# Reordering the two ends of a Strassen-style MLP whose down products share one PSUM bank pair

## The reference, cut to what matters

```python
D_MODEL, SEQ, DEPTH, D_FF = 1024, 512, 2, 4096

def squared_relu_mlp(h, w1, w2):
    return jnp.square(jax.nn.relu(h @ w1)) @ w2

def reference(x, mem, ...):
    for i in range(DEPTH):
        h = rmsnorm(x, norm_mix_g[i])
        x = x + (pool_mixer(h, ...) if i % 2 == 0 else sgu_mixer(h, ...))
        h = rmsnorm(x, norm_mem_g[i])
        x = x + mem_attention(h, rmsnorm(mem, norm_memkv_g[i]), ...)
        h = rmsnorm(x, norm_ffn_g[i])
        x = x + squared_relu_mlp(h, ffn_w1[i], ffn_w2[i])
    return rmsnorm(x, final_norm_g)
```

## Time and profile before

| what | value |
|---|---|
| median of 3 runs | 1170.44 us (1170.16 to 1172.05) |
| profiled execution | 1171.35 us, its span 1169.3 us |
| PE busy | 1140.8 us, 98% of the span |
| DVE busy | 829.2 us, 71% |
| ACT busy | 635.7 us, 54% |
| chain that ended last | PE 82%, DVE 9%, DMA 3%, ACT 3%, issue 2% |

### The profile page before, as it was taken

The page is one execution under the profiler, slowest core; times in us unless marked ns, Lnnn a source line. Parts: engine busy times, 40 slices in busy tenths (PEclk is TensorE's granted clock), DMA queues, the critical chain, the costliest instruction groups (busy, mean ns, idle before and its releaser), DMA issues.

```text
span 1169.3 us, 16188 instructions
## 1 busy us (share of the span) xinstructions
PE 1140.8 (98%) x6556; PEld 1003.9 (86%) x6556; DVE 829.2 (71%) x933; ACT 635.7 (54%) x773; POOL 251.3 (21%) x211
## 2 busy tenths in 40 slices
PE   8999999999999999999999999999989999999997
PEld 6888888989999999788888888888989999999975
DVE  7787647677786786777487656655757678677778
ACT  7664434765555655545444432543576656556555
POOL 0040035113012121113164044004511211112020
PEclk9999999999999999999999999999999999999999
DMA  9523134969789777735232622313587977977673
GB/s 349 206 80 101 55 135 107 244 133 192 196 181 201 186 143 164 174 73 198 91 97 84 216 91 72 108 36 144 118 227 158 198 191 179 207 171 154 146 133 102
DMA packets 48457, 176.59 MB, mean 151 GB/s; under 512 B 5504, under 2 KB 5632, under 8 KB 47744
## 3 DMA queue, kind: packets, MB, share of 16 engines
q0 software_dynamic: 18432, 67.12, 31.9%
q1 hardware_dynamic: 28368, 104.35, 26.5%
q10 hardware_dynamic: 1584, 4.10, 1.0%
HBM read 173.45 MB, written 2.10 MB: 150 GB/s over the span
## 4 chain that ended last, share of the span: by engine, by line
PE 82%; DVE 9%; DMA 3%; ACT 3%; issue 2%; POOL 0%; SPq 0%; DVEq 0%; ACTq 0%; POOLq 0%
PE psum L1874 11%; PE psum L1876 11%; PE psum L1875 11%; PE psum L2149 8%; PE psum L2150 8%; PE psum L2151 8%; PE psum L2129 8%; PE psum L2131 7%; PE psum L2130 7%; DVE w_lo L1181 2%; DMA w_raw<-in_up 2%; DMA w_raw<-in_weights 1%; DVE w_lo L1170 1%; PE psum L2066 1%; ACT w_hi L725 1%
## 5 line engine op out<-in xcount | busy, mean ns | idle before, releaser
L1181 DVE TENSOR_TENSOR w_lo<-w_sum,w_hi 128x1024 fp32r<-128x1024 f32 x112 | 136.5, 1223 | 84.2 <-ACT w_hi L725 83.9
L2149 PE MATMUL psum<-w_lo,slot_hi 128*128 128x512 f32 x448 | 176.3, 394 | 5.2 <-DVE y_rows L1519 5.2
L2150 PE MATMUL psum<-w_hi,slot_hi 128*128 128x512 f32 x448 | 176.3, 393 | 0.0
L2151 PE MATMUL psum<-w_hi,slot_lo 128*128 128x512 f32 x448 | 175.6, 392 | 0.0
L725 ACT ACTIVATE w_hi<-w_sum 128x1024 fp32r<-128x1024 f32 x112 | 117.7, 1054 | 79.8 <-PE psum L2151 76.0
L2129 PE MATMUL psum<-xs_s_lo,w_hi 128*128 128x256 f32 x512 | 145.4, 284 | 0.9 <-DVE a L1457 0.8
L2131 PE MATMUL psum<-xs_s_hi,w_lo 128*128 128x256 f32 x512 | 144.9, 283 | 0.0
L2130 PE MATMUL psum<-xs_s_hi,w_hi 128*128 128x256 f32 x512 | 144.8, 283 | 0.0
L1827 POOL DMA_DIRECT2D w_sum<-in_down x64 | 55.4, 866 | 373.5 <-DVE w_lo L1181 373.5
L1181 DVE TENSOR_TENSOR w_lo<-w_raw,w_hi 128x1024 fp32r<-128x1024 f32 x80 | 101.0, 1265 | 48.7 <-ACT w_hi L725 48.4
L725 ACT ACTIVATE w_hi<-w_raw 128x1024 fp32r<-128x1024 f32 x80 | 83.9, 1056 | 80.0 <-PE psum L2131 64.1
(11 more groups left out here) (226 smaller groups left out, 2701.1 us busy)
## 6 DMA issues: line engine op xcount, KB each, us to landing
w_raw<-in_weights SPq DMA_DIRECT2D x90, 512.0 KB, 3.7
w_sum<-in_down POOLq DMA_DIRECT2D x64, 512.0 KB, 6.9
w_sum<-in_down SPq DMA_DIRECT2D x48, 512.0 KB, 4.5
w_raw<-in_up POOLq DMA_DIRECT2D x48, 512.0 KB, 6.4
w_raw<-in_up SPq DMA_DIRECT2D x32, 512.0 KB, 3.9
up<-in_up SPq DMA_DIRECT2D x16, 512.0 KB, 4.3
up<-in_up POOLq DMA_DIRECT2D x16, 512.0 KB, 7.2
x<-in_x_t SPq DMA_DIRECT2D x2, 1024.0 KB, 8.8
```

The lines of the kernel that those rows point to most:

```text
L1181: dve.tensor_tensor(w_lo[:, c % RING, :], buffer(kind, SUM_BUFFER[STAGE[p][0]] + half), w_hi[:, c % RING, :].bitcast(F32), ALU.subtract).t ...
L2149: pe.matmul(to, s_hi[:, k, tok], w_lo[:, c % RING, cols], start=first, stop=False, skip_group_check=True)
L2150: pe.matmul(to, s_hi[:, k, tok], w_hi[:, c % RING, cols], start=False, stop=False, skip_group_check=True)
L2151: last = pe.matmul(to, s_lo[:, k, tok], w_hi[:, c % RING, cols], start=False, stop=(kp == 1 and j == 1), skip_group_check=True)
```

## The change

There are four parts. (1) In block 0, on VectorE, `c11`, the halves of `c12` and those of `c22` each move ahead of one weight split. On ScalarE the squares of a12 and a22 move behind the next weight split. SyncE issues its first DMAs of the MLP in another order. (2) The up products of block 3 are done sooner: at the end of block 2 the order was D2P6, U3P6, D2P7, U3P7, D2P4, U3P4, and it is now U3P6, D2P6, U3P7, U3P4, D2P7, D2P4 (`LAST_UPS`). The work on a12, a22, a21 and the sums s1 to s4 moves with them, and the read of D2P4 moves into the last block. (3) In the last block D3P3 gets bank pair A for itself instead of adding onto D3P5 in pair Y. (4) So D3P5 is read a second time, into the quarter of `y_rows` that D3P3 belongs to. The halves of the tile-by-tile read of D3P5 are gone. The count of matmuls, of weight chunks and of bytes is the same.

```diff
+LAST_UPS = (("D", "P1"), ("U", "P1"), ("D", "P2"), ("U", "P2"), ("D", "P5"), ("U", "P5"), ("D", "P3"), ("U", "P3"),
+            ("U", "P6"), ("D", "P6"), ("U", "P7"), ("U", "P4"), ("D", "P7"), ("D", "P4"))
-LAST_READS = ("P1", "P5", "P3", "P6", "P2", "P7", "P4")
+LAST_READS = ("P1", "P5", "P5 again", "P3", "P6", "P2", "P7", "P4")
...
-    for b in range(FB - 1):
+    for b in range(FB - 2):
         for p in ORDER:
             steps += [("D", b, p, h) for h in range(2)] + [("U", b + 1, p, h) for h in range(2)]
+    steps += [(kind, FB - 2 + (kind == "U"), p, h) for kind, p in LAST_UPS for h in range(2)]
...
 def rows_pair(b, p):
-    return PAIR_E if (b, p) == (FB - 1, "P2") else ROWS_PAIR[p]
+    if b == FB - 1 and p in ("P2", "P3"):
+        return PAIR_E if p == "P2" else PAIR_A
+    return ROWS_PAIR[p]
...
@@ SyncE, start of an MLP @@
-                refill(l, "U", 0, "P2")
                 sp.wait_ge(lo_ready, N.lo[f"xs{l}", "P4"] + 1)
-                for name in ("11", "22"):
-                    for half in range(2):
-                        quarter(l, "D", 0, name, half)
-                refill(l, "U", 0, "P7")
+                for half in range(2):
+                    quarter(l, "D", 0, "11", half)
                 refill(l, "U", 0, "P4")
+                refill(l, "U", 0, "P2")
+                for half in range(2):
+                    quarter(l, "D", 0, "22", half)
+                refill(l, "U", 0, "P7")
@@ ScalarE, block 0 @@
-                squared(0, 1, a12, "P6")
                 ahead("U", 0, "P7", 1)
+                squared(0, 1, a12, "P6")
+                ahead("U", 0, "P4", 0)
                 operand(0, "P2", a12, h=1)
-                ahead("U", 0, "P4", 0)
+                ahead("U", 0, "P4", 1)
                 squared(0, 2, a22, "P7")
-                ahead("U", 0, "P4", 1)
@@ ScalarE, end of block 2 @@
+                ahead("D", b, "P7", 0)
+                last_quarter(c)
+                ahead("D", b, "P7", 1)
+                ahead("D", b, "P4", 0)
+                operand(c, "P2", a12, h=1)
+                ahead("D", b, "P4", 1)
                 b = FB - 1
-                last_quarter(b)
@@ VectorE, end of block 2 @@
+                ahead("U", c, "P4", 1)
+                ahead("D", b, "P7", 0)
+                sum_s1(c)
+                ahead("D", b, "P7", 1)
+                sum_s3(c)
+                sum_s2(c)
+                ahead("D", b, "P4", 0)
+                read(b, "P7")
+                operand(c, "P2", a12)
+                ahead("D", b, "P4", 1)
+                sum_s4(c)
                 b = FB - 1
-                sum_s1(b)
                 ahead("D", b, "P1", 0)
-                sum_s3(b)
                 operand(b, "P5", s1)
+                read(b - 1, "P4")
                 ahead("D", b, "P1", 1)
-                sum_s2(b)
-                sum_s4(b)
+                operand(b, "P3", a12)
                 ahead("D", b, "P2", 0)
-                operand(b, "P3", a12)
                 read(b, "P1")
                 ahead("D", b, "P5", 0)
-                read(b, "P5", tile_waits=True)
                 ahead("D", b, "P5", 1)
                 operand(b, "P6", a11)
                 ahead("D", b, "P3", 0)
+                read(b, "P5")
                 ahead("D", b, "P3", 1)
+                read(b, "P5", again=True)
                 read(b, "P3")
@@ TensorE, end of block 2 @@
+                kept_done(c, "P1")
+                up_product(c, "P6")
+                read_done(b, "P1")
+                down_product(b, "P6")
+                sum_done(c, "P6")
+                up_product(c, "P7")
+                pe.wait_ge(sum_half, 3 * l + 3)
+                up(c, "P4", 0)
+                sum_done(c, "P7")
+                up(c, "P4", 1)
+                read_done(b, "P6")
+                down_product(b, "P7")
+                read_done(b, "P7")
+                down_product(b, "P4")
                 b = FB - 1
                 read_done(b - 1, "P4")
                 down_product(b, "P1", fresh=True)
                 kept_done(b, "P3")
                 down(b, "P2", 0, fresh=True).then_inc(psum_ready, 1)
                 read_done(b - 1, "P3")
                 down_product(b, "P5", fresh=True)
-                waits = [read_count(l, b, "P5", t) for t in range(2)]
-                down(b, "P3", 0, tile_waits=waits).then_inc(psum_ready, 1)
-                down(b, "P3", 1).then_inc(psum_ready, 1)
+                kept_done(b, "P4")
+                down_product(b, "P3", fresh=True)
                 read_done(b, "P1")
```

More of the change, by code:

```diff
@@ L593, in read_count @@
         order = LAST_READS if b == FB - 1 else READS
-        return 14 * (FB * l + b) + 2 * order.index(p) + t + 1
+        return 14 * (FB * l + b) + 2 * l + 2 * order.index(p) + t + 1
     TOK = (slice(0, NMEM), slice(NMEM, S))
@@ L1015, in mlp @@
                     ahead("U", c, "P4", 1)
+                ahead("U", c, "P6", 0)
+                keep_p3(c)
+                ahead("U", c, "P6", 1)
+                ahead("D", b, "P6", 0)
+                ahead("D", b, "P6", 1)
+                squared(c, 1, a12, "P6")
+                ahead("U", c, "P7", 0)
+                operand(c, "P1", a11, h=0)
+                ahead("U", c, "P7", 1)
+                ahead("U", c, "P4", 0)
+                squared(c, 2, a22, "P7")
+                ahead("U", c, "P4", 1)
[5 more added lines that the diff above has]
+                ahead("D", b, "P4", 1)
                 b = FB - 1
-                last_quarter(b)
                 ahead("D", b, "P1", 0)
@@ L1499, in sum_s4, with read @@
                                              op1=ALU.subtract).then_inc(s_step, 1)
-                def read(b, p, tile_waits=False):
-                    i, j = ROWS_PART[p]
-                    before = PART_BEFORE[p]
+                def read(b, p, tile_waits=False, again=False):
+                    i, j = ROWS_PART["P3" if again else p]
+                    before = PART_BEFORE["P3" if again else p]
+                    if (b, p) == (FB - 1, "P3"):
+                        before = "P5 again"
                     order = LAST_READS if b == FB - 1 else READS
-                    if before in order[:order.index(p)]:
+                    if before in order[:order.index("P5 again" if again else p)]:
                         dve.wait_ge(rows_read, read_count(l, b, before))
@@ L1559, in mlp @@
                 ahead("U", 0, "P6", 0)
-                ahead("U", 0, "P6", 1)
                 dve.wait_ge(ssq_step, SUMMED[norm])
                 c12(0, half=0)
+                ahead("U", 0, "P6", 1)
+                c12(0, half=1)
                 ahead("U", 0, "P7", 0)
-                c12(0, half=1)
                 row_scales()
+                c22(0, half=0)
                 ahead("U", 0, "P7", 1)
-                c22(0, half=0)
+                c22(0, half=1)
+                ahead("U", 0, "P4", 0)
                 operand(0, "P2", a12)
-                ahead("U", 0, "P4", 0)
-                c22(0, half=1)
                 ahead("U", 0, "P4", 1)
@@ L1622, in mlp @@
                     ahead("U", c, "P4", 1)
+                ahead("U", c, "P6", 0)
+                ahead("U", c, "P6", 1)
+                c12(c)
+                ahead("D", b, "P6", 0)
+                ahead("D", b, "P6", 1)
+                ahead("U", c, "P7", 0)
+                read(b, "P6")
+                operand(c, "P1", a11)
+                c22(c, half=0)
+                ahead("U", c, "P7", 1)
+                c22(c, half=1)
+                ahead("U", c, "P4", 0)
+                ahead("U", c, "P4", 1)
+                ahead("D", b, "P7", 0)
[8 more added lines that the diff above has]
+                sum_s4(c)
                 b = FB - 1
-                sum_s1(b)
                 ahead("D", b, "P1", 0)
-                sum_s3(b)
                 operand(b, "P5", s1)
+                read(b - 1, "P4")
                 ahead("D", b, "P1", 1)
-                sum_s2(b)
-                sum_s4(b)
+                operand(b, "P3", a12)
                 ahead("D", b, "P2", 0)
-                operand(b, "P3", a12)
                 read(b, "P1")
                 ahead("D", b, "P5", 0)
-                read(b, "P5", tile_waits=True)
                 ahead("D", b, "P5", 1)
@@ L1835, in mlp @@
                     for p in ("P1", "P5", "P3", "P6"):
+                        if (b, p) == (FB - 2, "P6"):
+                            add_quarters(l, "U", b + 1, p)
+                            add_quarters(l, "D", b, p)
+                            continue
                         add_quarters(l, "D", b, p)
@@ L2152, in down @@
                                              stop=(kp == 1 and j == 1), skip_group_check=True)
-                        if (b, t, kp) == (FB - 1, 0, 1) and p in ("P5", "P7"):
+                        if (b, t, kp) == (FB - 1, 0, 1) and p == "P7":
                             last.then_inc(tile_ready, 1)
@@ L2219, in mlp @@
                 wait_split((f"xs{l}", "P4"))
```

(1 more changed line is left out.)

19 lines of the change are left out of this document (12 added, 7 removed).

## The result

| | before | changed |
|---|---|---|
| median of 4 runs | 1171.14 us | 1184.13 us |
| lowest to highest | 1170.16 to 1172.05 | 1183.78 to 1184.17 |
| span of the profiled execution | 1169.3 us | 1182.2 us |
| mean granted clock of TensorE | 0.993 | 0.987 |

The changed kernel is slower: the ratio of the times is 1.0114, 95% interval 1.0098 to 1.013, which is 13.0 us by the medians and 12.9 us by the spans. The prediction was 10.6 us slower.

A forecast was written before the change was run, and what follows sets the result against it. TensorE was taken as the bound, busy 33.66 of 33.66 us around block 2's end. Added 29.0 less removed 18.4 gave +10.6 us: 1171.35 becomes 1182.0 us (median 1181.0), range 1174.5 to 1190.

The forecast's parts named there:

- (a) to (c): Block 0: earlier a11, a12 and a22 sums remove TensorE waits of 2.3, 0.8 and 3.9 us, plus 3.0 slow clock.
- (c): Block 0: a22's first half ahead of a late-weight split removes the 3.9 us "issue" wait and 2 x 1.5 slow clock.
- (2): Rival, block 0: the start gives nothing back, only (d) is won; +20.6 us, 1191 us; chance 0.05.
- (4): Rival, block 0: gains of (a) to (c) only move to the next late-weight wait; about +17, 1187 us; chance 0.06.
- (d): Last block: D3P3 no longer adds onto D3P5's banks, removing 5.2 us of wait and 2 x 1.6 of slow clock.
- The wait that the prediction said would prove it wrong: Last block: a new TensorE wait between D3P6 and D3P7, VectorE being 1.4 us further behind; not in the sum.
- The gaps: End of block 2: D2P4 and D3P1 each wait for VectorE's read of the product before, 6.0 and 5.1 us per MLP.
- The 0.2 us ahead of U3P4: End of block 2: up product P4 of block 3 starts late for a22's first half, 0.2 us per MLP.
- The slow clock: Behind each new gap, at D2P4 and D3P1: slow matmuls cost 1.6 us each, 3.2 per MLP.
- (3): Rival, D2P4 and D3P1: clock does not recover between gaps 7 us apart; 11.2 more, 1192 us; chance 0.10.
- (1): Rival, end of block 2: reads are prompt, gaps 1.75 us; -11.4 us, 1159 us; chance 0.07.

The follow-up runs named there:

- the start alone: Kernel before with only block 0's reordering on SyncE, ScalarE and VectorE: 1158.49 us, 10.9 less than the kernel before.
- the engines alone: Kernel before with only ScalarE's and VectorE's block 0 reordering, SyncE's queue left as it was: 1158.44 us, 11.8 less than the kernel before.
- both reads at once: Changed kernel with VectorE's reads of D2P7 and D2P4 moved ahead of the splits and sums before them: 1160.01 us, 10.2 less than the kernel before.
- Filling the waits: Changed kernel with unused 512-column matmuls, 22 behind D2P7 and 16 behind D2P4: 1175.29 us, 5.1 over the kernel before; with 18 and 16, 1176.35.

## Why the prediction was right in sign and 2.4 us short

- **Start, (a) to (c): 10.0 us predicted, 11.0 by the trace, 10.9 by the run with the start alone.** Right, and the claim in (c) that late weights don't matter once a22's half stands ahead of the split was shown by the run with the engines alone. SyncE's part, which the prediction expected to help if anything, adds nothing to theirs. Rivals (2) and (4) fall with the start alone, which keeps all it wins.
- **Last block, (d): 8.4 us predicted.** Against the kernel with both reads at once, which has neither the wait nor a slow clock there, the kernel before takes 44.81 - 40.64 = 4.2 us more from D3P1's start to the next layer's short wait (479.95 to 524.76 against 478.15 to 518.79), and in the second MLP 50.7 - 47.3 + 0.9 = 4.3 more up to the span's end (the 0.9 is the wait at D3P4, booked apart): 8.5. The size is right; there is luck in it as far as it counts on the clock falling behind both waits of the kernel before, which it did in that trace and in the start alone only once. The wait that the prediction said would prove it wrong, between D3P6 and D3P7, is real: it is in the kernels without the new order of block 2 (1.5 to 1.9 us). In the changed kernel it does not appear, but VectorE's delay shows one product later, 0.88 us at D3P4, a term that the sum did not have.
- **The gaps: 6.0 and 5.1 us predicted, 5.5 and 4.9 measured.** The chain was the right one, link by link (last quarter, s1, split, s3, s2, split, read). Only the weights were earlier than I had them: VectorE's split waits 0.27 us, where I had put down 0.9 for them. The 0.2 us ahead of U3P4 is there, as 0.25. Together 22.6 predicted, 21.2 measured, and 1.1 us for stopping and starting, which no row of before had shown me apart.
- **The slow clock: 1.6 us behind each gap predicted; this is the step that was mis-sized.** D2P4 takes 482.78 - 475.07 = 7.71 us and 8.23 in the second MLP; in the kernel with both reads at once 5.76 and 5.73. D3P1 to the same later points takes 2.4 and 2.7 us more than there. That is 2.0 + 2.5 + 2.4 + 2.7 = 9.6 us, not 6.4. I had taken the 1.6 from behind waits of 2 to 2.7 us. Behind those in the first MLP, the first matmul still ran at full clock or nearly (0.48 us; 0.62 in the second MLP); behind the waits of some 5 us it is slow from the first on (0.79), and the clock comes back 4.0 to 5.7 us after the start, which before was 3.7. Filling the waits showed the cost as one of its own: 9.1 us of span, 7.9 by the differences to before.
- **The rivals.** (3), a clock that does not recover, is refuted: D2P4 and D3P1 both end at full clock. (1), prompt reads at 1159 us, did not happen in this kernel, but its price was right: moved on VectorE alone, the reads give 1160.0. What decided against it was what I named, the work ahead of the two reads.

The sum's misses are 3.2 for the clock, 1.1 for stopping and starting and 0.9 at D3P4, less 1.4 in the gaps, 1.0 at the start and 0.1 in the last block: +2.7, against 2.3 by the spans (12.9 - 10.6) and 2.4 by the medians. That the total came so near is in part luck, since misses of both signs cancel.

The Trainium skill, "TensorE: Matmul & The Clock Gate", section "Why this matters for your kernels", speaks against long idle gaps between bursts of matmuls, as they send the engine back to half rate. The trace agrees on the new waits of 4.9 to 5.5 us: the granted clock is 0.50 behind them, and 1.00 when 22 and 16 matmuls leave at most 1.24 us of each. In this kernel the clock also fell behind gaps of 1.81 to 2.69 us, though not each time, and those are shorter than the ones that the page warns of.

## What to carry to other kernels

When products that share a bank are put next to each other, the price is the time from a product's end to the end of its read; look first at what stands ahead of that read in the reading engine's order. Here two reads moved on VectorE were worth 24 us, and the order of the products on TensorE then cost 3.3 (1157.9 against 1154.6 of span). A stall of TensorE can have two prices, the wait and the slow matmuls behind it. Cut from 5.5 or 4.9 us to 1.57, the stalls here lost the second price wholly and most of the first, while a stall moved to the next product saved nothing.
